# Raw first pair of groups with the norm factor applied to its banks, weight roundings between norm pieces and evictions, and the rounding of the gated tiles on ScalarE

## What is computed

```python
def rms_norm(x, g):
    xf = x.astype(F32)
    y = xf * lax.rsqrt(jnp.mean(xf * xf, axis=-1, keepdims=True) + NORM_EPS)
    return (y * g.astype(F32)).astype(x.dtype)

# first model, per layer
u = rms_norm(h, norm_mix_g[layer]);  p = u @ w_in[layer]
...
h = h + merged @ w_o[layer]
u = rms_norm(h, norm_ffn_g[layer])
h = h + conv_glu(u, w_up, conv_w, conv_b, w_down)   # (silu(gate) * val) @ w_down

# second model, per layer
h = rms_norm_2(x, g_mix_norm);  proj = h @ w_in
...
x = x + mix @ w_out
h2 = rms_norm_2(x, g_mlp_norm)
x = x + jnp.square(jax.nn.relu(h2 @ w_up)) @ w_down
```

## Time and profile before

| | |
|---|---|
| median of 3 runs | 2054.72 us (2047.13 to 2056.26) |
| profiled execution: time, span | 2048.42 us, 2046.5 us |
| granted TensorE clock, mean | 0.959 |
| TensorE matmuls / weight loads busy | 1883.6 us (92%) / 1778.9 us (87%) |
| DVE / ACT / POOL busy | 1293.0 (63%) / 1140.5 (56%) / 1037.9 (51%) |
| DMA | 271.20 MB, 133 GB/s |

### The profile page before, as it was taken

How to read it: one execution, slowest core, us unless ns; L and a number is a source line. 1 busy time by engine, 2 the same in 40 slices (tenths; PEclk the granted TensorE clock), 3 DMA queues, 4 the chain that set the end, 5 groups by cost and what they waited for, 6 DMA issues and landing times.

```text
span 2046.5 us, 44566 instructions
## 1 busy us (share of the span) xinstructions
PE 1883.6 (92%) x16390; PEld 1778.9 (87%) x16390; DVE 1293.0 (63%) x1943; ACT 1140.5 (56%) x1924; POOL 1037.9 (51%) x742
## 2 busy tenths in 40 slices
PE   8889889999999889888999999988899998879999
PEld 8778779999999778778999989866899997669999
DVE  3487725669913397824669963476786536777764
ACT  5653455456755654445557755665555457465544
POOL 5663449839986573448929985741200045411000
PEclk9999989999999999979999999997999999779999
DMA  6432015656665432005656664420366653205665
GB/s 208 122 103 71 23 39 158 176 145 186 188 187 164 124 114 74 23 22 154 176 151 179 187 173 133 150 89 21 112 183 202 193 166 113 72 17 154 186 193 173
DMA packets 146922, 271.20 MB, mean 133 GB/s; under 512 B 16433, under 2 KB 16946, under 8 KB 146738
## 3 DMA queue, kind: packets, MB, share of 16 engines
q1 hardware_dynamic: 145296, 264.97, 45.2%
q10 hardware_dynamic: 1442, 3.66, 0.5%
HBM read 267.52 MB, written 1.05 MB: 131 GB/s over the span
## 4 chain that ended last, share of the span: by engine, by line
PE 65%; DVE 15%; ACT 9%; POOL 8%; issue 3%; DMA 0%; ACTq 0%; DVEq 0%; SPq 0%
PE bank L649 63%; POOL ring_split L1317 8%; ACT arena L1351 7%; ACT hi_ring L1351 1%; PE bank L758 1%; DVE arena L1891 1%; DVE u L1961 1%; DVE arena L1890 1%; DVE arena L2062 1%; DVE arena L1975 1%; DVE arena L1974 0%; DVE arena L2109 0%; DVE arena L1973 0%; ACT L1351 0%; DVE arena L2464 0%
## 5 line engine op out<-in xcount | busy, mean ns | idle before, releaser
L1317 POOL TENSOR_TENSOR ring_split<-ring,hi_ring 128x512 fp32r<-128x512 f32 x682 | 969.1, 1449 | 736.7 <-ACT hi_ring L1351 730.9
L1351 ACT ACTIVATE hi_ring<-ring 128x512 fp32r<-128x512 f32 x1002 | 619.3, 630 | 555.1 <-PE bank L649 532.0
L649 PE MATMUL bank<-u_hi,hi_ring 128*128 128x256 f32 (+1 forms) x2480 | 676.1, 285 | 47.3 <-POOL ring_split L1317 39.7
L649 PE MATMUL bank<-u_split,hi_ring 128*128 128x256 f32 (+1 forms) x2480 | 665.4, 281 | 1.6 <-DVE u_split L1966 1.4
L649 PE MATMUL bank<-u_hi,ring_split 128*128 128x256 f32 (+1 forms) x2480 | 665.0, 281 | 0.0
L649 PEld LDWEIGHTS bank<-u_hi,hi_ring 128*128 128x128 f32 (+1 forms) x2480 | 452.3, 188 | 61.8 <-POOL ring_split L1317 41.1
L649 PEld LDWEIGHTS bank<-u_split,hi_ring 128*128 128x128 f32 (+1 forms) x2480 | 452.4, 188 | 4.0 <-DVE u_split L1966 2.4
L649 PEld LDWEIGHTS bank<-u_hi,ring_split 128*128 128x128 f32 (+1 forms) x2480 | 452.2, 188 | 0.9
L1999 DVE TENSOR_TENSOR ring_split<-ring,hi_ring 128x512 fp32r<-128x512 f32 x320 | 215.3, 694 | 111.9 <-ACT hi_ring L1351 108.1
L649 PE MATMUL bank<-arena 64*64 64x64 f32 (+6 forms) x3680 | 240.3, 255 | 14.6 <-DVE arena L2109 9.3
L649 PEld LDWEIGHTS bank<-arena 64*64 64x64 f32 (+3 forms) x3680 | 210.4, 155 | 49.5 <-issue 29.7
(11 more groups left out here) (246 smaller groups left out, 2407.0 us busy)
## 6 DMA issues: line engine op xcount, KB each, us to landing
ring<-in_stream SPq DMA_DIRECT2D x1002, 256.0 KB, 2.8
par<-in_params ACTq DMA_DIRECT2D x3, 637.0 KB, 4.3
h<-in_x SPq DMA_DIRECT2D x4, 256.0 KB, 4.3
cst<-in_cst SPq DMA_DIRECT2D x1, 993.0 KB
out<-h ACTq DMA_DIRECT2D x3, 256.0 KB, 2.8
par<-in_params ACTq DMA_DIRECT2D x1, 633.0 KB, 8.3
out<-h ACTq DMA_DIRECT2D x2, 128.0 KB, 2.3
msk<-in_masks SPq DMA_DIRECT2D x1, 104.0 KB
```

Of the source, the lines that this page charges most:

```text
L649: ins = nc.tensor.matmul(o, l, r, start=start, stop=stop)
L1317: G.tensor_tensor(ring_lo[:, c, :], ring[:, c, :], hi_ring[:, q % HI_RING, :].bitcast(F32), ALU.subtract).then_inc(lo_by_pool, 1)
L1351: return nc.scalar.activation(o, i, f, **kw)
```

## The change

At every norm boundary the first pair of groups is now computed from raw tiles, `h * g` without the norm factor. ACT writes the high part of `h * g` (`raw_high`) part by part behind the squares, DVE the low part (`raw_low`) behind its add. `project_raw` starts on them, and `norm_total` stands between its tiles k = 1 and k = 2. The filler matmuls of the boundary go. The normed tiles, made meanwhile into the same buffers as TensorE lets go of the raw ones (`raw_used`), serve a second pair, `project_normed`. DVE multiplies the two raw banks by the factor (`rescale`; in the second model as part of the relu or of the copy out). The table of weights gets a third stretch of two pieces that DVE owns and six that POOL owns. The roundings of weights are put between the norm pieces and, for pieces 14 to 16 behind a boundary, between the first evictions.

In the first model's feed-forward loop the rounding into `hidden_hi` moves to ACT, one turn later, and DVE subtracts one turn later still; at the last turns two single roundings of weights are put around the silu. The norm that joins the models gets its two totals behind k = 1 and k = 2.

```diff
-BY_VECTOR1 = {"A second", "WO", "U second"}
-BY_VECTOR2 = {"cq second", "WO", "U second", "D"} | {f"U{i}" for i in range(2, 16)}
+BY_VECTOR1 = {"A second", "A third", "WO", "U second", "U third"}
+BY_VECTOR2 = {"cq second", "cq third", "WO", "U second", "U third", "D"} | {f"U{i}" for i in range(4, 16)}
...
-                norm_total("norm2", squares, 0)
                 last = l + 1 == layers[0]
-                project_first(("U0", "U1"), 5, 8)
-                for i in range(2, 22):
+                project_raw(("U0", "U1"), past, lambda k: norm_total("norm2", squares, "sums_ready", past["sums_ready"] + 1) if k == 1 else None)
+                project_normed([("U2", 0), ("U2", T), ("U3", 0), ("U3", T)], 5)
+                for i in range(4, 22):
                     project(f"U{i}", 2, u_parts)
...
+            def raw_high(C, gain, part_):
+                for k in range(part_.start, part_.stop):
+                    ins = A(u_hi[:, k, :], h[:, k, :], ACT.Copy, scale=gain[:, k:k + 1])
+                C.link(ins, S["raw_hi"])
...
@@ last_squares
                     C.link(A(dst[:, part_, :], h[:, part_, :], ACT.Square), S["squares_ready"])
...
+                    raw_high(C, gain, part_)
                     if last and j == 1:
                         act.wait_ge(S["cum_ready"], past["cum_ready"] + 2)
                         C.link(A(tab, tab, ACT.Sin), S["decay_ready"])
...
@@ norm_hi
                     C.link(A(u_hi[:, part_, :], u[:, part_, :], ACT.Copy), S["u_hi_ready"])
-                    if j > 1:
-                        hi.make(at + HI_RING + j - 1)
+                    hi.make(at + (8, 10, 11, 13, 14)[j])
...
@@ the first model's feed-forward loop on ACT
-                for i in range(23):
+                for i in range(24):
                     if i < 22:
                         hi.upto(f"U{i}")
                         bank = B.wait(act, f"U{i}")
+                        if i < 2:
+                            hi.upto(LAST_WO[-1], 16 + i)
+                            act.wait_ge(S["raw_scaled"], past["raw_scaled"] + 2 + i + 1)
...
-                    if i:
+                    if i in (21, 22):
+                        hi.more()
+                    if 0 < i < 23:
                         act.wait_ge(S["conv_mid"], past["conv_mid"] + i)
                         C.link(A(cb[(i - 1) % 4][:, 0, :], cb[(i - 1) % 4][:, 0, :], ACT.Silu), S["conv_out"])
+                    if i == 22:
+                        hi.more()
+                    if i > 1:
+                        act.wait_ge(S["hidden_in"], past["hidden_in"] + i - 1)
+                        C.link(A(hidden_hi[:, i - 2, :], hidden[:, i - 2, :], ACT.Copy), S["hidden_high"])
...
+            def raw_low(C, gain, part_, n):
+                dve.wait_ge(S["raw_hi"], past["raw_hi"] + n)
+                for k in range(part_.start, part_.stop):
+                    ins = V.scalar_tensor_tensor(u_lo[:, k, :], h[:, k, :], gain[:, k:k + 1], u_hi[:, k, :].bitcast(F32), ALU.mult, ALU.subtract)
+                C.link(ins, S["raw_lo"])
...
@@ add_last
                     B.release(dve, name)
-                    if sums and j in (1, 2):
+                    if gain is None:
+                        continue
+                    if j in (1, 2, 4):
                         dve.wait_ge(S["squares_ready"], past["squares_ready"] + 5 * which + j + 1)
...
+                    raw_low(C, gain, part_, 5 * which + j + 1)
...
@@ norm_parts
-                    if j > 2:
-                        lo.make(at + HI_RING + j - 2)
+                    lo.make(at + HI_RING + j + 3)
+
+            def rescale(C, B, names):
+                for name in names:
+                    bank = B.wait(dve, name)
+                    C.link(V.tensor_tensor(v3(bank[:, :], 2), v3(bank[:, :], 2), spread(rn[:], 2), ALU.mult), S["raw_scaled"])
```

299 lines of the change are left out of this document (167 added, 132 removed).

## The result

| | before | changed |
|---|---|---|
| median, 20 runs each, same chip | 2051.3 us | 2064.12 us |
| ratio, 95% interval | | 1.0049 [1.0033, 1.0065] |
| profiled execution: time, span | 2048.42, 2046.5 us | 2059.18, 2057.1 us |

The account below looks back on a forecast made before the run. TensorE, busy 92% of the span, was taken as the bound, with waits for DVE, ACT or POOL to be won. Terms 4.2 + 6.1 + 4.8 + 2.1 − 1.7 + 3.6 + 3.8 − 7.5 + 6.0 = 21.4 gave 2033 us, range 2020 to 2044.

Parts of the forecast that it names:

- the second model's feed-forward boundary: Twice in the second model: 5.2 us to win less 3.4 charged for late DVE work, 1.8 gained each, 3.6 for both.
- Its own list of what would show it wrong: U turns without wait (then 2026), second model's WO behind by under a microsecond (2028), or wait per turn near .85.
- its signs: What the changed kernel's trace should show, including second-model totals waiting 2.3 us for sums and the clock staying at its higher level.
- First model's feed-forward boundary: Twice in the first model: 4.8 less 1.3 for a POOL wait and .45 in WO, 3.05 us gained each, 6.1 both.
- D of the second layer: First model's layer 2: raw_high on ACT ahead of the decay table costs .9 us, later parts .8, 1.7 lost.
- The U loop: First model's feed-forward loops: ACT's rounding delays POOL past its slack, .22 us a turn, 17 turns, two loops, 7.5 lost.
- Loops' ends: End of the first model's U loops: single roundings around the silu remove both 2.86 us waits for POOL, 6.0 gained.
- between the models: Norm joining the models: a 10.17 us hole, but a long chain of totals and second norm, so 2.1 gained.
- the mixer boundaries: Boundaries before each model's second mixer: 4.8 us gained in the first model, 3.8 in the second.
- The head: Kernel start: raw tiles need only the input loads ahead of TensorE, so the first pair ends sooner, 4.2 us gained.
- C: Rival: serial ACT and DVE chains, .2 more per link, and raw tiles meeting POOL cost 13 us; 2046, chance .13.
- D: Rival: ACT's U-loop rounding makes POOL a whole piece late, TensorE waiting 1.37 us in each of 34 turns; 2072, chance .08.

Follow-up runs that it names:

- e5: Changed kernel with the two totals at the second model's feed-forward boundary behind raw tile k = 3 instead of k = 1; 1.0065 to the kernel before.
- e6: Changed kernel with the low parts of pieces 17 and 18 made ahead of U1's squares on DVE in the second model; 1.0071 to the kernel before.
- e7: Changed kernel with six filler matmuls put back at the second model's feed-forward boundary, in the wait for the sums; 1.0043 to the kernel before.
- e9: Changed kernel with the second model's two feed-forward boundaries as in the kernel before, everything else as changed; 1.0004 to the kernel before.
- e12: Kernel before with only the first model's feed-forward rounding into hidden_hi moved to ACT and DVE's subtraction a turn later; 1.0074 to the kernel before.
- e11: Changed kernel without DVE's raw low parts in the second model's WO (results not what they should be); 1.0046 to the kernel before.
- e10: Changed kernel with the old form at the second model's feed-forward boundaries plus queue-order repairs that held; 2039.61 against 2047.23 us, 0.9962 to the kernel before.

## Why the prediction was wrong, point by point

**The step that failed first: the second model's feed-forward boundary.** The forecast had 5.2 to win less 3.4 charged, 1.8; 4.2 were lost. The time of a part was right (4.6 forecast, 4.45 measured), the charges made from it were not. It charged 1.1 for the last WO piece, the row says 2.36 idle (2.5 by the starts); 2.3 for the totals, measured 2.84 (3.0). It had no term for the 17th piece, whose low part stands on DVE behind the last normed tiles and two rescaled and squared groups (2.44; before, that piece did not wait). And its sum had no term for the clock: 7 us for it stood in its range alone, and its signs had the clock staying up. It fell twice, and by the starts 1.7 and 1.5 us are lost behind the two falls. Against all this the hole gave 6.6 and not 5.2 (.86 is taken off twice in the sum, the second time without a reason), and a wait of the twelfth piece, .77 before, went. Its own list of what would show it wrong counted only better cases for this step. e5, e6 and e7 show why no single edit mended it: a wait or a fall of the clock that is taken away comes back as a wait at a later piece. e9 shows that undoing it is worth the loss of the whole change. How the lateness is shared between the round trips over ACT and DVE's slower work beside POOL is open.

**First model's feed-forward boundary.** 3.05 each was forecast, .4 and .5 came. The fourth piece behind the second pair waited 2.28, not 3.4, so that term was even too dear. But the ninth and tenth pieces were charged .5 and one waited 1.41; WO waited .86 where .45 was charged; the second piece before it waited .60 for POOL, uncharged. Every wait costs .16 more than its idle column says, since the row's matmul is modelled .28 long and starts are .12 apart.

**D of the second layer.** The forecast charged raw_high on ACT in front of the table load (.9). The real price was one step earlier: raw_low of the first part waits 3.02 for ACT, and behind it on DVE stand 17 us of angles. The prediction asked what is queued behind the waiting instruction, but not at this place, and it priced no instruction of DVE but raw_low as longer beside POOL. +5.3 for +1.7.

**The U loop.** Place and cause were right, the size not: .22 a turn forecast, .30 measured. The slack was reckoned on one piece; in the trace two pieces of each turn hesitate, and at each the matmul after the late one is spaced .19 too. That the rest of the chain (e12, 15 us alone) is larger still stayed hidden in the changed kernel because its two single roundings mend D's first pieces.

**Loops' ends, between the models, the mixer boundaries.** -2.6 for -6.0: the wait of 2.86 went, as said, and 1.47 stands at the third piece after it. -1.2 for -2.1, -3.6 for -4.8 and -2.8 for -3.8: signs and mechanism right, each short by the tenth piece's wait of 1.67 to 1.97, where .5 was charged for the ninth. The head's −3.9 for −4.2 is luck: 4.1 were won by the ninth piece, 1.7 of it went at the tenth (idle 1.48), and the 1.5 that make up the figure came later, where the clock happened to be low in the execution before. Also 28.9 − 24.0 is 4.9 and not 4.8, which moves the sum by some .4.

**The rivals.** C, serial chains over ACT and DVE and raw tiles that meet POOL, comes nearest to what happened. It was sized at 1.6 more a boundary; at the second model's it is 6. By its .2 per link it was thought of as small delays added, while the loss is whole waits. D, a whole piece late in each U turn, did not happen. The slower side came from C, for which the prediction had allowed no result above the kernel before. On the rule of the Trainium skill, "SBUF — State Buffer", section "Who interferes with whom": the changed kernel's trace agrees. The rows above have DVE's copy at 1.41 beside POOL and .43 alone, its instruction of two inputs at 2.96 for two and .88, and POOL's pieces took 1.79 each beside the angles and 1.24 each while DVE stood by:

```profile
1221.60 5.38 POOL L1315 TENSOR_TENSOR ring_split<-ring,hi_ring 128x512 fp32r<-128x512 f32 x3
1233.49 3.73 POOL L1315 TENSOR_TENSOR ring_split<-ring,hi_ring 128x512 fp32r<-128x512 f32 x3 [6.51 <-ACT hi_ring L1349]
```

The forecast looked for this at raw_low in D. The trace has it where the new order puts POOL's pieces beside other work of DVE: at the last normed tiles (5.2 us) and at the angles (17.3 for 13.8). e11 says nothing on it, since it takes away raw low parts that run while POOL mostly stands still. So this stays a rival in part untested.

## What to carry to other kernels

Filler in front of a boundary is a hole that can be filled only if the work put there is ready without a round trip between two engines; where a part's time over such a round trip (4.5 us) exceeds the matmuls beside it (2.8), the hole comes back at a later piece, whichever wait was removed here. Before moving pieces to an idle engine, look at what they will now run beside. Before adding an instruction that waits, list what stands behind it on its own queue at every place where the shared helper is called. And test a part of a change alone: here one moved rounding cost 15 us by itself and one kind of boundary 9, and with these two put right the rest was worth having (e10).

## What the runs showed of the hardware

**Two spacings at one clock.** In some stretches matmuls of this form start every .118 us, in others every .113, with a granted clock of 1.00 in both. The same stretch of the second model's D, before and then changed (columns as above):

```profile
1600.00:1650.00 50.00, 50.00 (x444) 50.00 (x443) 27.19 (x41) 24.99 (x40) 1.29 (x1) 1.00 0.69 193
```

```profile
1600.00:1650.00 50.00, 50.00 (x427) 49.81 (x426) 28.44 (x44) 25.26 (x42) 0.00 (x0) 1.00 0.64 186
```

444 matmuls against 427 in 50 us without a wait. In the kernel before 2464 matmuls of the profiled execution have the short spacing, in the changed one 1553; at .0045 us each that is 11 against 7 us, so some 4 of the 10 us between these two executions, and most of the rows "D loops" in the table. In the kernel before it lasts through D in both layers of the second model, from the first matmul on; in the changed one it starts there too in the first of them, stops where TensorE hesitates for .2 us and comes back later, and in the last D it is missing. It doesn't belong to D: in e9 it stands in the second model's U loops and ends with the first matmul of D. What sets it I could not settle, and no run tried it. It may be part of why executions of one kernel differ by up to 1.3% here, and it is why a table of two traces can't be read to a single microsecond.

**A fall of the clock cost 1.5 to 1.7 us** by the starts of the matmuls, at each of the four places of the second model, and what follows it decides whether they can be won back: e7 removed one fall in each layer and kept .15 and nothing.

**The whole difference is as large as the clock's.** The mean granted clock of the 20 runs of the changed kernel is .954; of the kernel before, in the runs beside the experiments, .958 to .959, and of e9 .959. With the two levels of 1.2 and 2.4 GHz this is 189 us at the lower one against some 170. If TensorE had work in all of the 19 us, half of them would be lost, 9 to 10 us: my estimate, and an upper bound. In the two profiled executions it is 182 against 167, and the four falls behind new waits make up nearly all of the 15 more. It is no separate cause, then, and e7 says that a fall taken away alone gives nothing.
